# One 3 MB transfer per expert, instead of 2 MB and 1 MB, in the expert loop of a two-layer transformer trunk

## The reference, cut to what matters

```python
h = rmsnorm(x, norm_ffn_g[l]) * (1.0 + sc2) + sh2
y = swiglu(h2, w_shared_gu[l], w_shared_down[l]) + moe_routed(h2, router_w[l], router_bias[l],
                                                              w_exp_gu[l], w_exp_down[l])
x = x + g2 * y
# moe_routed: scores = sigmoid(h2 @ router_w); the 6 best of 64 experts per token;
# for each expert e, on its tokens: (silu(g) * u) @ w_down[e], with g, u = split(h @ w_gu[e]);
# the results, weighted by the normalised scores, are summed per token
```

## Time and profile before

| what | us |
|---|---|
| three runs: median (lowest to highest) | 3065.34 (3057.83 to 3067.11) |
| the profiled execution: its time | 3058.53 |
| the profiled execution: its span | 3056.9 |
| PE busy, of the span | 2849.8 (93%) |
| DVE busy | 2034.1 (67%) |
| ACT busy | 1583.1 (52%) |
| POOL busy | 647.7 (21%) |

### The profile page before, as it was taken

The page is one execution under the profiler, slowest core; times in us unless marked ns, Lnnn a source line. Parts: engine busy times, 40 slices in busy tenths (PEclk is TensorE's granted clock), DMA queues, the critical chain, the costliest instruction groups (busy, mean ns, idle before and its releaser), DMA issues. The chain is left out here.

```text
span 3056.9 us, 42263 instructions
## 1 busy us (share of the span) xinstructions
PE 2849.8 (93%) x13740; PEld 2172.8 (71%) x13740; DVE 2034.1 (67%) x2885; ACT 1583.1 (52%) x2482; POOL 647.7 (21%) x563
## 2 busy tenths in 40 slices
PE   5999998899799999999779999989998999999994
PEld 4677776677577777777556777766776777777773
DVE  4544446555588888888845444565546888888886
ACT  2342433433357777777533334244324777777772
POOL 0100000100035653333210000001001356433330
PEclk9999999999899999999889999999998999999997
DMA  7224342233569999999712243412425999999985
GB/s 231 76 75 147 117 138 90 80 118 131 199 250 359 361 372 367 358 368 357 278 60 78 93 142 116 152 63 95 144 91 195 365 358 353 362 373 365 360 321 224
DMA packets 124556, 671.47 MB, mean 220 GB/s; under 512 B 27628, under 2 KB 29036, under 8 KB 90444
## 3 DMA queue, kind: packets, MB, share of 16 engines
q1 hardware_dynamic: 91040, 605.91, 54.0%
q0 software_dynamic: 31424, 57.44, 5.6%
q10 hardware_dynamic: 1932, 6.16, 0.9%
HBM read 656.60 MB, written 55.28 MB: 233 GB/s over the span
## 5 line engine op out<-in xcount | busy, mean ns | idle before, releaser
L2136 DVE TENSOR_TENSOR ew_lo<-ew,e_hi 128x2048 fp32r<-128x2048 f32 x258 | 591.7, 2293 | 183.9 <-ACT e_hi L1935 183.9
L1935 ACT ACTIVATE e_hi<-ew 128x2048 fp32r<-128x2048 f32 x260 | 497.6, 1915 | 79.0 <-PE bank L2342 79.0
L707 PE MATMUL bank<-h_hi,w_hi 128*128 128x512 f32 x1248 | 510.6, 409 | 27.0 <-DVE w_lo L641 10.5
L707 PE MATMUL bank<-h_hi,w_lo 128*128 128x512 f32 x1248 | 502.9, 403 | 0.0
L707 PE MATMUL bank<-h_lo,w_hi 128*128 128x512 f32 x1248 | 500.8, 401 | 0.0
L641 DVE TENSOR_TENSOR w_lo<-raw,w_hi 128x1024 fp32r<-128x1024 f32 x198 | 242.2, 1223 | 318.8 <-ACT w_hi L633 318.3
L2342 PE MATMUL bank<-e_hi,x_hi 128*128 128x512 f32 x1040 | 418.2, 402 | 0.1
L2342 PE MATMUL bank<-ew_lo,x_hi 128*128 128x512 f32 x1040 | 407.5, 392 | 0.0
L2342 PE MATMUL bank<-e_hi,x_lo 128*128 128x512 f32 x1040 | 405.3, 390 | 0.0
L1825 POOL DMA_INDIRECT y_d<-y,idx x130 | 224.9, 1730 | 513.0 <-issue 423.3
L707 PEld LDWEIGHTS bank<-h_hi,w_hi 128*128 128x128 f32 x1248 | 239.6, 192 | 106.2 <-issue 36.4
(11 more groups left out here) (317 smaller groups left out, 4398.1 us busy)
## 6 DMA issues: line engine op xcount, KB each, us to landing
ew<-in_wexp SPq DMA_DIRECT2D x130, 2048.0 KB, 9.6
raw<-in_wmix SPq DMA_DIRECT2D x297, 512.0 KB, 3.4
ew<-in_wexp SPq DMA_DIRECT2D x130, 1024.0 KB, 9.7
ew<-y_d SPq DMA_DIRECT2D x8, 2048.0 KB, 11.8
ew<-y_d SPq DMA_DIRECT2D x8, 1024.0 KB, 8.3
ada0a<-in_ada SPq DMA_DIRECT2D x2, 2048.0 KB, 13.4
ada0b<-in_ada SPq DMA_DIRECT2D x2, 2048.0 KB, 22.2
h_d<-htok ACTq DMA_DIRECT2D x8, 512.0 KB, 12.4
```

The source lines that it names most:

```text
L707: ins = nc.tensor.matmul(out, lhs, rhs, start=start, stop=stop)
L1935: nc.scalar.activation(e_hi[h][:], up_part(ew, j, h), ACT.Copy).then_inc(whi_done, 1)
L2136: nc.vector.tensor_tensor(up_part(ew_lo, j, h), up_part(ew, j, h), e_hi[h][:].bitcast(F32), ALU.subtract).then_inc(wlo_done, 1)
```

## The change

The two loads of an expert become one load of 3 MB, which signals `gw_in[j]`; `dw_in` and ACT's two waits for it are gone. The load of expert `e` is issued when `down(e - 4)` is done, where the down load stood; the wait for `gu_used` is gone. At the end of the stage the read of the overflow list comes to stand behind the 3 MB load of place 60 in SP's queue; before it was ahead of the gate and up load of place 61 and of the down load of place 60.

```diff
-                    load_up(0, 0)
-                    load_down(0, 0)
-                    load_up(1, 1)
-                    load_down(1, 1)
+                    def load_expert(e, j):
+                        sp.dma_start(ew[j][:], wexp_d[l * NE + e]).then_inc(gw_in[j], 16)
+
+                    load_expert(0, 0)
+                    load_expert(1, 1)
                     load_tile(sp, l, MIX_TILES + RAW)
-                    load_up(2, 2)
-                    load_down(2, 2)
+                    load_expert(2, 2)
...
                     sp.wait_ge(mark, shared_mark)
-                    load_up(3, 3)
-                    load_down(3, 3)
-                    sp.wait_ge(gu_used, 2)
-                    load_up(4, 0)
+                    load_expert(3, 3)
                     with sp.Fori(1, NE // 4 - 1) as it:
                         for j in range(4):
-                            sp.wait_ge(gu_used, 8 * it + 2 * j - 4)
-                            load_up(4 * it + j + 1, (j + 1) % 4)
                             sp.wait_ge(dn_ready, 4 * it + j - 3)
-                            load_down(4 * it + j, j)
+                            load_expert(4 * it + j, j)
...
                     for j in range(4):
                         e = NE - 4 + j
-                        sp.wait_ge(gu_used, 2 * e - 4)
+                        sp.wait_ge(dn_ready, e - 3)
+                        load_expert(weights_of(e), j)
                         if e + 1 == OV:
                             sp.wait_ge(y_out[OV % 4], 16 * ((OV - 8) // 4 + 1))
                             sp.dma_start(idx[OV % 8][:].unsqueeze(1), slot_rows[BLK:2 * BLK, bass.ds(over, 1), :]).then_inc(over_in, 16)
-                        load_up(weights_of(e + 1), (j + 1) % 4)
-                        sp.wait_ge(dn_ready, e - 3)
-                        load_down(weights_of(e), j)
                     sp.wait_ge(dn_ready, NE - 3)
-                    load_down(weights_of(NE), 0)
+                    load_expert(weights_of(NE), 0)
...
-                        act.wait_ge(dw_in[j % 4], 16 * (2 * it + j // 4 + 1))
...
-                            act.wait_ge(dw_in[0], 16 * (NE // 4 + 1))
```

More of the change, by code:

```diff
@@ L417, in hybrid_trunk @@
         gw_in = [sem(f"gw_in{i}") for i in range(4)]
-        dw_in = [sem(f"dw_in{i}") for i in range(4)]
         xg_in = [sem(f"xg_in{i}") for i in range(4)]
```

## The result

The changed kernel takes 3135.18 us (median of 4 runs, 3130.64 to 3147.13) against 3062.39 us before: a ratio of **1.024, 95% interval 1.0219 to 1.0261**. It is 73 us slower; the forecast was 3 us slower, in a range up to 3084. The profiled execution took 3131.2 us, with a span of 3129.6.

The account below looks back on a forecast made before the run. PE was taken to pace the expert stages, with loads early. Late weights 0.5 us plus the list stall 2.2 us made 2.7 us on the median 3065.3: 3068.0 us, with an 8-in-10 range from 3056 to 3084.

Parts of the forecast that it names:

- What bounds the kernel: Expert stages: PE sets the pace at 9.7 us an expert, loads are early, no weight wait to remove.
- The lead: Expert loop: 3 MB needed 13.4 us after issue, usually landing in 12.7 us; late landings cost 0.5 us.
- The overflow list: End of stage: list lands behind place 60's load; PE stalls 2.2 us in layer 1, 0 in layer 2.
- things priced at nothing: Prologue, SP's issues, ACT's `dw_in` wait, end reads and gather waits (-3 to +3 us): all taken as 0.
- Rival 2: Expert loop becomes bound by loads landing later than 14.9 us in many steps: 3090 or 3110 us; chance 0.17.
- Rival 3: Expert stages: gather waits go, -3.6 us, and no list stall, 3062 us; chance 0.13 (with any gain).

Follow-up runs that it names:

- experiment 5: Changed kernel with weights in 8 KB pieces and the overflow list read ahead of the load of place 60: 3065.89 us, ratio 1.0007 to the kernel before.
- experiment 11: Changed kernel with weights in 4 KB pieces and the overflow list read ahead of the load of place 60: 3065.65 us, ratio 1.0011.
- experiment 2: Changed kernel, still one 3 MB issue, with weights laid out in DRAM as 8 KB pieces: 3072.32 us, ratio 1.0033.
- 6: Changed kernel, still one 3 MB issue, with weights laid out in DRAM as 12 KB pieces: 3097.06 us, ratio 1.0097.
- 9: Changed kernel with the slot rows written a second time in places 24 to 47: 3174.6 us, ratio 1.0363.
- 10: Kernel before with 4 KB pieces and the slot rows written a second time in places 24 to 47: 3054.43 us, ratio 0.9973.
- 7: Changed kernel with the 3 MB as two 1.5 MB issues, even and odd partitions, rows still 24 KB: 3139.33 us, ratio 1.0241.
- experiment 1: Changed kernel with each expert's 3 MB as two issues (2 MB and 1 MB) back to back at the late point: 3085.19 us, ratio 1.0073.
- 4: Kernel before, two issues at early and late point, with weights in 8 KB pieces: 3055.9 us, ratio 0.9977.
- 8: Kernel before, two issues, with weights in 4 KB pieces: 3047.76 us, ratio 0.9952.

## Why the prediction was wrong

- **What bounds the kernel: right.** PE paces the loop in the kernel before, and nothing could be won.
- **The lead: right for the changed kernel, with some luck.** 13.4 us were allowed and 12.7 expected; the 3 MB land in 11.7 us. In the changed kernel's loop from 1050 to 1450 us ACT waited 2.6 us in all for weights, and PE never for `ew_lo`. But that loop stood 56 us for rows, in which the loads had time. Where it hardly stands and the pieces are smaller (experiment 5, 3 MB in 13.1 us), ACT waits 62.5 us for weights and PE 4.0 us for `acted`, in experiment 11 6.4 us: the 0.5 us of this term would have been too little there.
- **The overflow list: right in mechanism, taken too small.** It landed 13.4 and 11.8 us after its issue (worked out: 12.7 and a little), POOL waited 17.3 us for it in two layers, and PE stood 3.6 us in the first and at most 1.5 us in the second (2.2 and 0 in the sum). By the ratios of experiments 2 and 5 the list costs 8 us (3 to 13), more than the 2.2 that I took.
- **The step that failed** stands among the things priced at nothing: "The 3.6 us of gather waits may shrink or grow with the new timing of the loads: -3 to +3, taken as 0." It measured +52.8 us, and 18.6 us of PE's busy time at the lower clock behind it, which no term had. I treated the row transfers as sharing bytes with the loads, and the bytes were the same. What they share goes by packets, and the change halved the number of the load's. The changed kernel, 6 and 2 against each other (packet size alone, with issue point and transfer count held) and 9 against 10 (the same demand beside big and small packets) show it; 7 shows that the transfers' number and size do nothing. That an engine takes its queues in turn, one packet each, is the reading that fits and is not itself shown: a row packet that waits for a fixed number of load packets already on their way would be late in the same measure.
- **Rival 2** named the right side and came nearest in size (3110 against 3135), but by the wrong wait: it had the weights late. Rival 3 named the right wait with the wrong sign; what stood against it, "the same bytes", is the error of the forecast.
- **What the rows of before did hold.** The queue's line on the page gives packets beside bytes, and I read the bytes only. The gathers land 9.3 us after their issue, and PE starts on their rows 11.7 us after it (medians of 130; one was issued at 1445.96 and needed at 1457.77). Read one by one, half of them had 1.1 us or less to spare, where the weights had some 10 (20.1 less 9.6). The three short waits in the earlier trace rows were where this margin had run out.

Of the 73 us, then: about 50 are the merged packets (changed kernel less experiment 1). The other 22 are the list, about 8 (experiment 2 less 5), and the late issue point. This last stays with small packets too: 9 us with 24 packets (experiment 5 less 4) and 18 us (12 to 25) with 48 (experiment 11 less 8), where the 3 MB also land later. Part of it is seen, as PE's waits for rows and for `acted`. Why rows are late at the late point even beside small packets is open; that the load then goes out as one burst in which the gather of that step also runs would fit, and was not tested.

## What to carry to other kernels

Joining two transfers of adjacent columns joins their packets: look at the packet count beside the bytes, and divide it by the rows. A queue of small packets beside a queue of big ones gets on the more slowly, the bigger those are, so give bulk loads pieces near the size of the small queue's (4 KB here; with 2 KB the loads landed 19.1 us after their issue instead of 10.7, and the gain was gone) by laying them out apart in DRAM, even where the bulk load is in no hurry. For a change that delays nothing that PE waits for, find the transfer with the smallest margin, whoever issued it, and ask what the change does to that one.

## What the hardware showed that I had not expected

- Transfers to 64 adjacent partitions each ran at 207 GB/s, where 64 alternate ones kept the rate of the changed kernel (341 GB/s from 900 to 1300 us, and 9.7 us for 1.5 MB against 21.3).
- The size of the pieces of a 1 MB load, 8 KB, 4 KB, 2 KB, gave landings of 9.6, 10.7 and 19.1 us. The DMA share from 2500 to 2900 us was 0.99 with 4 KB and 1.03 with 2 KB, at 363 and 358 GB/s: the loads queue up once the engines are full.
- After an idle stretch of 4.8 us the matmuls ran at a granted clock of 0.57 for some 4 us. Over all 27 waits of the changed kernel that made 18.6 us on 56.4, a third on top; in experiment 1, with 18 waits of 2.4 us at most, the clock stayed at 1.00 in both stages.
